# Rounded weight halves placed by their number among the split units, and the token rows' fetch put ahead of the scatters on GpSimd

## What is computed

```python
def ffn(args):
    xb, e = args
    return (jax.nn.silu(xb @ w1[e]) * (xb @ w3[e])) @ w2[e]
...
out = jnp.einsum('nkd,nk->nd', y.reshape(n_tok, TOP_K, d), e_w.astype(y.dtype))
```

## Time and profile before

| | us |
|---|---|
| median of three runs | 2134.13 |
| the profiled execution | 2134.49 |
| its span, first to last instruction | 2132.7 |
| TensorE busy | 2049.1 (96%) |
| VectorE busy | 1555.0 (73%) |
| ScalarE busy | 1192.5 (56%) |
| GpSimd busy | 135.7 (6%) |
| mean of the DMA over the span | 288 GB/s |

### The profile page before, as it was taken

How to read it: one execution, slowest core, us unless ns; L and a number is a source line. 1 busy time by engine, 2 the same in 40 slices (tenths; PEclk the granted TensorE clock), 3 DMA queues, 4 the chain that set the end, 5 groups by cost and what they waited for, 6 DMA issues and landing times.

```text
span 2132.7 us, 27841 instructions
## 1 busy us (share of the span) xinstructions
PE 2049.1 (96%) x10774; PEld 1669.2 (78%) x10774; DVE 1555.0 (73%) x1498; ACT 1192.5 (56%) x967; POOL 135.7 (6%) x92
## 2 busy tenths in 40 slices
PE   8999999999999999999999999999999999999996
PEld 8998888899999998887887767667777666766663
DVE  7656664453646375454769999999999999999987
ACT  5445653333333323334346777777777777777773
POOL 1000000000000000001000111011110111011010
PEclk9999999999999999999999999999999999999998
DMA  6554335655454544667779999999999999999993
GB/s 215 158 140 158 118 119 185 209 181 170 147 177 146 169 157 155 220 216 256 227 286 366 410 426 427 426 427 427 424 426 426 420 422 422 417 415 421 410 426 159
DMA packets 143693, 613.47 MB, mean 288 GB/s; under 512 B 19057, under 2 KB 31489, under 8 KB 116257
## 3 DMA queue, kind: packets, MB, share of 16 engines
q1 hardware_dynamic: 137760, 601.14, 73.2%
q0 software_dynamic: 5856, 11.26, 1.5%
HBM read 612.87 MB, written 24.13 MB: 299 GB/s over the span
## 4 chain that ended last, share of the span: by engine, by line
PE 64%; DMA 12%; DVE 11%; issue 8%; ACT 3%; POOL 1%; POOLq 0%; DVEq 0%; ACTq 0%
PE ps L2023 18%; PE ps L2004 15%; DMA raw<-in_w_dram 7%; DVE wl L801 6%; PE ps L1152 5%; PE ps L1153 5%; DMA xrows<-xscr,rowno 4%; PE ps L2381 4%; PE ps L1149 4%; ACT wh L641 2%; DVE yall L973 2%; PE ps L2136 2%; PE ps L1174 1%; PE ps L2096 1%; PE ps L2109 1%
## 5 line engine op out<-in xcount | busy, mean ns | idle before, releaser
L801 DVE TENSOR_TENSOR wl<-raw,wh 128x2048 fp32r<-128x2048 f32 x320 | 720.4, 2286 | 72.0 <-ACT wh L641 71.0
L641 ACT ACTIVATE wh<-raw 128x2048 fp32r<-128x2048 f32 x320 | 604.4, 1912 | 184.6 <-PE ps L1153 82.0
L1578 DVE TENSOR_TENSOR wl<-raw,wh 128x2048 fp32r<-128x2048 f32 (+1 forms) x168 | 379.7, 2263 | 286.5 <-ACT wh L1382 286.4
L1382 ACT ACTIVATE wh<-raw 128x2048 fp32r<-128x2048 f32 (+1 forms) x168 | 317.9, 1894 | 447.4 <-DMA raw<-in_w_in_dram 276.4
L1152 PE MATMUL ps<-wh,xg 128*128 128x512 f32 x776 | 329.8, 425 | 33.7 <-DVE wl L801 33.4
L1153 PE MATMUL ps<-wl,xg 128*128 128x512 f32 x776 | 303.7, 391 | 0.0
L2004 PE MATMUL ps<-hth,wh 128*128 128x272 f32 (+1 forms) x896 | 259.7, 290 | 3.2 <-DVE wl L1578 1.8
L2004 PE MATMUL ps<-htl,wh 128*128 128x272 f32 (+1 forms) x896 | 255.8, 285 | 0.0
L2004 PE MATMUL ps<-hth,wl 128*128 128x272 f32 (+1 forms) x896 | 255.5, 285 | 0.0
L1149 PE MATMUL ps<-raw,xg 128*128 128x512 f32 x496 | 222.9, 592 | 0.0
L1152 PEld LDWEIGHTS ps<-wh,xg 128*128 128x128 f32 x776 | 145.9, 188 | 86.0 <-DVE wl L801 38.3
(11 more groups left out here) (369 smaller groups left out, 2918.0 us busy)
## 6 DMA issues: line engine op xcount, KB each, us to landing
raw<-in_w_dram SPq DMA_DIRECT2D x192, 2048.0 KB, 16.9
raw<-in_w_in_dram SPq DMA_DIRECT2D x103, 1024.0 KB, 5.1
raw<-in_w_pa_dram SPq DMA_DIRECT2D x16, 1024.0 KB, 5.0
raw<-in_w_pb_dram SPq DMA_DIRECT2D x16, 1024.0 KB, 5.1
raw<-in_w_out_dram SPq DMA_DIRECT2D x16, 1024.0 KB, 5.1
raw<-in_w_ukv_dram SPq DMA_DIRECT2D x8, 1024.0 KB, 5.4
yscr<-zeros SPq DMA_DIRECT2D x4, 1024.0 KB, 8.4
yrow<-yscr SPq DMA_DIRECT2D x4, 1024.0 KB, 19.6
```

What stands on the lines that cost most here:

```text
L641: nc.scalar.activation(wh2[:, x % HELD, :], raw_of(turn, x), ACT.Copy).then_inc(s_wh2, 1)
L801: nc.vector.tensor_tensor(wl_of(turn, x), raw_of(turn, x), wh2[:, x % HELD, :].bitcast(F32), ALU.subtract).then_inc(s_wl2, 1)
L1382: nc.scalar.activation(wh[:, n % RING1, 0:c], raw1[:, n % RING1, 0:c], ACT.Copy).then_inc(s_wh, 1)
L1578: nc.vector.tensor_tensor(wl[:, n % RING1, 0:c], raw1[:, n % RING1, 0:c], wh[:, n % RING1, 0:c].bitcast(F32), ALU.subtract).then_inc(s_wl, 1)
```

## The change

It has two parts. Places in `wh2` are given by the number of a unit among the split units (`X_SPLIT`), not by the unit's own number, and at split unit x of the walk the halves of the fourth split unit after it are made (`shifted`); at a whole unit none are made. And on GpSimd the fetch of the rows stands ahead of both scatters.

```diff
+        SPLITS = [x for x in range(24) if x not in XR]
...
+        def shifted(x, by):
+
+            n = len(SPLITS) * (x // 24) + X_SPLIT[x % 24] + by
+            return 24 * (n // len(SPLITS)) + SPLITS[n % len(SPLITS)]
+
+        def held(x):
+            return wh2[:, X_SPLIT[x % 24] % HELD, :]
...
                 with pool.Fori(first, end) as p:
+                    rows(p + 1, p)
                     scatter(p, 0)
-                    rows(p + 1, p)
                     scatter(p, 1)
...
             def hi(turn, x):
-                if whole(turn, x):
-                    return
                 landed2(act, turn, x)
-                if isinstance(turn, int) and 24 * turn + x <= HELD:
+                if isinstance(turn, int) and split_units(turn, x) < HELD:
                     act.wait_ge(s_wused, N_UNITS)
                 else:
-                    done(act, turn, x - HELD)
-                nc.scalar.activation(wh2[:, x % HELD, :], raw_of(turn, x), ACT.Copy).then_inc(s_wh2, 1)
+                    done(act, turn, shifted(x, -HELD))
+                nc.scalar.activation(held(x), raw_of(turn, x), ACT.Copy).then_inc(s_wh2, 1)
...
-                    if x + HELD != HELD or not early:
-                        hi(turn, x + HELD)
+                    if not whole(turn, x) and not (last and x == 19):
+                        hi(turn, shifted(x, HELD))
...
-                    lo(turn, x + HELD)
+                    if not whole(turn, x) and not (last and x == 19):
+                        lo(turn, shifted(x, HELD))
```

More of the change, by code:

```diff
@@ L797, in lo @@
             def lo(turn, x):
-                if whole(turn, x):
-                    return
                 dve.wait_ge(s_wh2, split_units(turn, x) + 1)
-                nc.vector.tensor_tensor(wl_of(turn, x), raw_of(turn, x), wh2[:, x % HELD, :].bitcast(F32),
+                nc.vector.tensor_tensor(wl_of(turn, x), raw_of(turn, x), held(x).bitcast(F32),
                                         ALU.subtract).then_inc(s_wl2, 1)
@@ L1151, in unit @@
                     else:
-                        nc.tensor.matmul(o, s, wh2[:, x % HELD, c:c + 512], start=st, stop=False, skip_group_check=True)
+                        nc.tensor.matmul(o, s, held(x)[:, c:c + 512], start=st, stop=False, skip_group_check=True)
                         m = nc.tensor.matmul(o, s, wl_of(turn, x)[:, c:c + 512], start=False, stop=sp_,
```

## The result

The changed kernel took **2140.29 us**, the median of seven runs (2138.49 to 2142.56), beside 2134.13 us (2131.88 to 2134.97) in seven runs of the kernel before: ratio 1.0032, 95% interval 1.0021 to 1.0044. It is slower by some 6 us. The forecast was 2135.0 us in a range of 2130.0 to 2139.5, and "no change that can be measured" had 0.75: 5 us too low, and outside the range by 0.8. The profiled execution took 2140.39 us with a span of 2138.5 us, 5.8 more than before.

The account below looks back on a forecast made before the run. The prediction took the DMA, not TensorE, to bound the kernel. First turn +1 and end -0.2, halves and fetch at nothing, gave +0.8 us on 2134.1, about 2135 us, range 2130 to 2139.5.

Parts of the forecast that it names:

- What bounds the kernel: From about 1190 us to the end of the weights: the DMA is the resource without a gap, late turns 61.2 us.
- the first rival: Later turns: TensorE sets the pace after all, so removed waits come off the time; 14.5 us faster, 2119.6 us, chance 0.07.
- The halves, priced at nothing: Steady turns: halves made one split unit earlier remove TensorE's waits for VectorE, but the DMA's backlog covers them; 0 us.
- The fetch, at nothing, issued 12 us ahead of the scatter: GpSimd, each turn: fetch issued some 12 to 14 us earlier removes TensorE's waits for `xrows`; backlog swallows it, 0 us.
- The first turn ... I take +1: First turn, DMA running dry: VectorE's steps come one subtraction later, TensorE some 2 us late; +1 us, bounds -1.8 and +4.
- The end, at -0.2: After the last weights: VectorE's subtractions and `product` same in number, only reordered; -0.2 us, bounds -2.3 and +2.3.
- the first turn's delays add up: TensorE reaches the second turn 4 us late or more, DMA runs dry once more; +5 us, 2139 us, chance 0.06.
- two at once make -4 to +5: Range: two of the three terms' bounds together, with 0.02 beyond the gain's 4.3 us and 0.03 beyond the loss's.

## Why the prediction was wrong

*What bounds the kernel* held. The DMA's share is 1.00 from 1180 to 2050 us, the late turns keep their length, loads passed 16 us to landing sooner than before, and 23 us of extra work on TensorE cost 2.2. So the first rival, TensorE sets the pace, was rightly kept low. With the middle turns alone new the time was the same, ratio 0.9995; this says less, since about half of TensorE's waits came back at `mix` and `hidden` (5.4 and 1.4 us, where 13.7 us had been). The Trainium skill (Perfetto Trace Analysis, Optimization Strategies) speaks of engines "that are blocking the critical path"; the prediction left these words out of its advice, and here the waits were not on that path.

*The halves, priced at nothing:* right for the 14 middle turns; in the last turn they can cost (below). The waits for subtractions and rows went, and others took their place. I had named `copy_up` among what queues behind a rounding that waits for a load, but followed `hidden` alone (3.1 us in three waits); `mix` was the one that waited.

*The fetch, at nothing, issued 12 us ahead of the scatter:* right as to both (12.7 us; ratio 0.9999 alone). Not foreseen: beside the halves it is needed, and saves 8.5 us. My sum treated the two parts as independent.

**The step that failed** is "The first turn ... I take +1, nearest to the one transposition that is on the path (2.3 us) less the fetch that fills in for it". The windows of the first turn make it 4.2 us, and the run with the new order there alone 4.6. The mechanism and the places were as told: the gather matrix late (1.60 us of wait against "up to 1.5"), `select` at 1153.13 where I had 1152.3, `mix` 2.8 us late. Five things in the term were wrong. I let only the last delay count, because the DMA's queue is never empty behind it; but each earlier delay also made a hole, at 1140 us and at 1160, and none was made up. The transposition I chose was not the one that decides. The fetch, which I let fill a hole, was issued at 1173.30, behind both. I took 2.3 us for one more subtraction, and the gather matrix came 3.4 us later, since that subtraction also waited for its rounding. And I did not price the clock: every row I had read showed 1.00, and TensorE had not stood for so long at that place before. That was 2.6 us by the run with the added matmuls, outside the sum and outside its bound of +4.

*The end, at -0.2:* of the wrong sign, but inside its bounds: in the changed kernel's profile it is 0.6 us. With the old first turn, the new last turn costs 2.8 us by the medians (2135.76 against 2132.97), by a wait at `mix` and the low clock behind it; this the term did not have.

*The rivals:* the one that came nearest was "the first turn's delays add up", 2139 us, and it had 0.06. Half of its condition, TensorE 4 us late or more, was met, with the clock's help. The other half, that the DMA runs dry once more in the second turn, was not: the holes lie ahead of it, in the first. So its figure came near in part by luck. The range has a slip of its own. The bounds of the terms reached +9 in sum, and I wrote that two at once make -4 to +5; two at once make 5.3 to 7.0 us on the slow side. With the largest pair the range would have ended at 2141.1 and held the result.

## What to carry to other kernels

Where a saturated queue follows a stretch in which it runs dry, price every hole of that stretch at its full length and add them up: nothing behind it gives time back, and nothing gained behind it counts. When an in-order engine is given work one step earlier, go through all that stands behind that work, in each turn that has an order of its own (the first, the last), and ask what each consumer does while it waits. Two edits that are each free can depend on each other: run the halves of a change alone and together.

## What was not expected of the hardware

A stand of TensorE of well under 2 us can cost more than itself. Behind 1.73 us the granted clock was 0.50 (the lower level, 1.2 GHz) for at least the 6 us from 1156 to 1162, worth 2.6 us more; behind 1.23 us (the run with the gather matrix moved) it fell as well, to 0.72 in the mean from 1154 to 1160. It does not follow each time: in the changed kernel a wait of 1.76 us at 1391 us was followed by 0.53, and one of the same 1.76 us at 1329 us by 1.00 in the six microseconds behind it; in the last turn 1.50 us were followed by 1.00, and 1.55 us with the old first turn by 0.50. The Trainium skill (TensorE: Matmul & The Clock Gate, HAM oscillation) tells of a kernel in which TensorE's waits for the DMA are followed by matmuls at the lower clock, turn after turn; the run with the halves alone agrees (0.79 where TensorE had waited 3.18 us for the token rows), and filling the wait with idle matmuls kept the clock at 1.00 and gave 4 us back. What remains open is why the same wait takes the clock down in one turn and not in another.
